# A two-part transformer kernel: expert weights in half-and-half slots with 512-column matmuls, gate slot first in the dense stages, and zero matmuls between stages

## The chip, the cores and the metric

One core of a Trainium2 chip (trn2) runs the whole program in one launch. The metric is the device time of one execution in microseconds (us). TensorE is called PE here, its weight loads PEld; VectorE is DVE, ScalarE is ACT, GpSimd is POOL, and SyncE (SP) issues the loads.

## What is computed

The input is x, 256 tokens of 1024 features, batch 1. The first block has two layers. Each layer is a feed-forward network, a mixer and a second feed-forward network, all of them behind an RMS norm whose shift, scale and output gate come from `silu(c) @ w_ada + b_ada` (nine vectors of 1024 per layer). The mixer of layer 0 is a differential attention of 4 heads beside a multiscale pooling; that of layer 1 is a short gated convolution. A feed-forward network is

```
x = x + 0.5 * g * ((silu(h @ wg) * (h @ wu)) @ wd)      # h = norm(x), wg, wu 1024 x 2816, wd 2816 x 1024
```

The second block has one layer: latent attention and block attention, two gates and an output projection, and then a mixture of experts: a router picks one of four groups for each token and two of the eight experts in it.

```
y[token] += weight * ((silu(h @ w_g[e]) * (h @ w_u[e])) @ w_d[e])   # w_g, w_u 1024 x 256, w_d 256 x 1024, 32 experts
```

A last norm gives the output. All data is float32.

## The kernel before

**Split precision.** Every product of a weight and an activation is three PE matmuls with float32r operands: high times high, high times low, low times high. ACT makes the high part of a weight tile (L1300, L1310, a copy to float32r), DVE the low part (L1678, L2213, raw minus high). PE needs both.

**Slots.** Weights go through three slots, s = 0, 1, 2, each with a raw tile, a high tile and a low tile of 128 x 2048 (1 MB). In a feed-forward network slot 0 holds a chunk of 256 columns of the gate weight, slot 1 the same of the up weight and slot 2 256 rows of the down weight; 11 chunks make a network. In the other dense stages unit u uses slot u mod 3. SP issues the load of a slot (`load`, L393 to L399) after it has waited until the previous content is split; semaphores `landed`, `high`, `split` and `used` count loads, high parts, low parts and matmuls done per slot. SP works through its loads in one written order, so that a load that waits holds those behind it. ACT and DVE also have written orders.

**Stages.** ffn0, mix0, ffn1, ffn2, mix1, ffn3, blk2, moe. ffn0 to ffn2 also load the 4 MB of w_ada for each vector in quarters (`ada_load`) and DVE reduces them (L1730). Ahead of each stage stands a norm: ACT squares x in four pairs of feature blocks as they become final (L1323), PE sums the squares over partitions with a matrix of ones (`norm_sums`, L683, matmuls at L690), ACT takes the root (L1329), DVE the reciprocal (L1744), and then for each of the eight feature blocks k of h: DVE scales (L1688), ACT makes hhi (L1337), DVE makes hlo (L1688 with hlo as output; L1772 where there is no shift) and counts `h_ready`.

**The start of a stage.** `first_two` (L603) does the first two units, or the first gate and up chunk. It waits for both slots before its first matmul. For each k, as h_ready comes, it does output half m=0 of slot 0 and of slot 1 (six matmuls of 256 columns); then half m=1 of slot 0 for all k (24 matmuls, then `used[0]`), and half m=1 of slot 1 (24 matmuls, then `used[1]`). In a feed-forward network 16 zero matmuls of 128 columns (L792) go ahead of it, which open the PSUM banks of the down product. After it the next gate chunk follows (L579 to L581 via `gate`), for which slot 0 must be refilled: ACT copies after `used[0]`, DVE subtracts, and only then does ACT apply silu to the first gate chunk.

**Loads ahead of ffn3.** The last four units of mix1 are in slots 0, 1, 2, 0. `chunk_loads` (L405) then loads the first gate chunk into slot 0 and after it the first up chunk into slot 1. ACT's `norm` (L1314 and on) makes high parts between the squares (`refill`, L1302): the last mix1 unit of slot 0, the first up chunk, the first down chunk; DVE makes the low parts between the output additions of mix1 (`add_units`, L1876 and on).

**The expert stage.** An expert's gate is in slot 0, its up in slot 1, its down in slot 2; the raw tiles exist twice (even and odd experts). `expert` (L490) issues three loads of 1 MB for each expert, in order gate, up, down, each with 8 KB contiguous per partition, after the split of the same slot two experts earlier. On PE an expert's tokens (128) are the stationary operand and the weights move. Per step (L1226 and on):

```
into_hidden(0, e + 1)    # gate: 8 row blocks x 3 matmuls of 256 columns, L1183 to L1185
hidden_turn(e)           # two transposes of silu * up, L1194
into_hidden(1, e + 1)    # up: 24 matmuls of 256 columns
out_of_hidden(e)         # down: 12 matmuls of 512 columns, L1208 to L1210
```

In three of eight steps of groups 1 to 3, `scatter` (L1223, L1224) adds 4 or 8 matmuls. ACT applies silu after `used[1]`, DVE multiplies by up and the slot weight.

## Time and profile before

| | us |
|---|---|
| median of 3 runs | 1722.42 (1721.34 to 1727.29) |
| the profiled execution, its own time | 1724.32 |
| its span | 1722.5 |
| PE busy in the span | 1609.0 |
| DVE busy | 1130.3 |
| ACT busy | 780.7 |
| moved by DMA | 379.90 MB |

The span is the time from the first to the last instruction of the profiled execution, and that execution's own time is 1.8 us more. A row of the timeline gives when an instruction starts and how long it lasts; matmuls overlap their successors, so what a matmul costs in a dense run is the distance from one start to the next and not its duration. In the windows view PEclk is the share of full speed that PE's clock was granted. Lines "L579" and so on are lines of the kernel above.

### The profile page before, as it was taken

Reading aid. Unit: us, or ns where it says so; the run is one execution under the profiler, and the core shown is the slowest. Engines: PE = TensorE matmul, PEld = TensorE weight load, DVE = VectorE, ACT = ScalarE, POOL = GpSimd, SP = SyncE. Lnnn points to the kernel's source line nnn. Section 1 sums busy time; section 2 is a strip of 40 time slices with the busy share of each in tenths; the row PEclk is TensorE's granted clock in tenths of the full one; section 3 lists DMA queues with packets and bytes.
Section 4 is the critical chain, followed back from the end, with each engine's and each line's share of the span. In section 5 each row is a group of like instructions: output and inputs, shape, how many; then the busy total and the mean of one; then the engine's idle time right before and its main releaser. Section 6 shows DMA issues by size and latency. Waiting matters only on the chain.

```text
span 1722.5 us, 29138 instructions
## 1 busy us (share of the span) xinstructions
PE 1609.0 (93%) x12267; PEld 1522.4 (88%) x12267; DVE 1130.3 (66%) x1156; ACT 780.7 (45%) x808; POOL 17.2 (1%) x24
## 2 busy tenths in 40 slices
PE   5999989789999999998988999899899889999995
PEld 3999988579999999998988999898788689999994
DVE  2777777567777677756645454664664568888983
ACT  2433344434333443334434333444454447777772
POOL 0000000300000000000000000000000000000000
PEclk8999999889999999999998999999999889999997
DMA  9897766336878587863625555354332518898980
GB/s 323 273 329 278 271 242 242 125 123 248 289 270 313 173 292 270 313 196 126 196 98 171 177 188 177 126 171 117 110 123 98 218 54 347 342 357 346 357 327 26
DMA packets 202482, 379.90 MB, mean 221 GB/s; under 512 B 12185, under 2 KB 157470, under 8 KB 190110
## 3 DMA queue, kind: packets, MB, share of 16 engines
q1 hardware_dynamic: 202398, 378.70, 62.4%
q8 instruction: 62, 1.02, 0.2%
q14 instruction: 22, 0.18, 0.0%
HBM read 377.63 MB, written 1.05 MB: 220 GB/s over the span
## 4 chain that ended last, share of the span: by engine, by line
PE 84%; DVE 7%; ACT 4%; DMA 3%; issue 1%; SPq 0%; ACTq 0%; DVEq 0%
PE ps L579 20%; PE ps L580 19%; PE ps L581 19%; PE ps L1183 3%; PE ps L1185 3%; PE ps L1184 3%; DVE wlo L1678 3%; ACT whi L1300 2%; PE ps L1208 2%; PE ps L1209 2%; PE ps L1210 2%; DMA ada_raw<-in_w_ada_dram 2%; PE ps L690 2%; DVE rstd L1744 1%; PE ps L705 1%
## 5 line engine op out<-in xcount | busy, mean ns | idle before, releaser
L1678 DVE TENSOR_TENSOR wlo<-raw,whi 128x2048 fp32r<-128x2048 f32 (+1 forms) x191 | 432.9, 2267 | 346.5 <-ACT whi L1300 346.4
L579 PE MATMUL ps<-hhi,whi 128*128 128x256 f32 (+1 forms) x2024 | 587.7, 290 | 27.8 <-DVE hlo L1688 16.7
L580 PE MATMUL ps<-hlo,whi 128*128 128x256 f32 (+1 forms) x2024 | 579.1, 286 | 0.0
L581 PE MATMUL ps<-hhi,wlo 128*128 128x256 f32 (+1 forms) x2024 | 578.7, 286 | 0.0
L1300 ACT ACTIVATE whi<-raw 128x2048 fp32r<-128x2048 f32 (+1 forms) x191 | 360.1, 1886 | 209.9 <-PE ps L581 164.2
L579 PEld LDWEIGHTS ps<-hhi,whi 128*128 128x128 f32 (+1 forms) x2024 | 395.1, 195 | 35.8 <-issue 26.5
L580 PEld LDWEIGHTS ps<-hlo,whi 128*128 128x128 f32 (+1 forms) x2024 | 395.1, 195 | 1.8 <-issue 1.4
L581 PEld LDWEIGHTS ps<-hhi,wlo 128*128 128x128 f32 (+1 forms) x2024 | 394.8, 195 | 0.0
L579 PE MATMUL ps<-hidhi,whi 128*128 128x256 f32 x704 | 201.0, 286 | 2.8 <-DVE wlo L1805 2.8
L581 PE MATMUL ps<-hidhi,wlo 128*128 128x256 f32 x704 | 199.2, 283 | 0.0
L580 PE MATMUL ps<-hidlo,whi 128*128 128x256 f32 x704 | 199.2, 283 | 0.0
L579 PEld LDWEIGHTS ps<-hidhi,whi 128*128 128x128 f32 x704 | 134.9, 192 | 9.4 <-issue 5.8
L580 PEld LDWEIGHTS ps<-hidlo,whi 128*128 128x128 f32 x704 | 135.0, 192 | 0.0
L581 PEld LDWEIGHTS ps<-hidhi,wlo 128*128 128x128 f32 x704 | 135.0, 192 | 0.0
L1730 DVE SCALAR_TENSOR_TENSOR arena<-ada_raw,cact,arena 128x1024 f32<-128x1024 f32 x98 | 125.8, 1284 | 3.4
L2213 DVE TENSOR_TENSOR wlo<-raw,whi 128x2048 fp32r<-128x2048 f32 x45 | 103.0, 2289 | 11.9 <-ACT whi L1310 11.0
L1365 ACT ACTIVATE hidhi<-act_tile 128x512 fp32r<-128x512 f32 x44 | 27.8, 632 | 169.8 <-DVE act_tile L1796 169.8
L1359 ACT ACTIVATE act_tile<-ps 128x512 f32<-128x512 f32 x44 | 26.3, 598 | 147.9 <-PE ps L581 147.8
L2213 DVE TENSOR_TENSOR wlo<-ada_raw,whi 128x2048 fp32r<-128x2048 f32 x32 | 73.3, 2291 | 24.1 <-ACT whi L1310 24.1
L579 PE MATMUL ps<-mhi,whi 128*128 128x256 f32 (+1 forms) x256 | 76.9, 300 | 12.4 <-DVE mlo L1899 8.8
L1310 ACT ACTIVATE whi<-raw 128x2048 fp32r<-128x2048 f32 x45 | 86.0, 1912 | 5.0 <-PE ps L1210 4.3
L580 PE MATMUL ps<-mlo,whi 128*128 128x256 f32 (+1 forms) x256 | 76.1, 297 | 0.0
(276 smaller groups left out, 2449.7 us busy)
## 6 DMA issues: line engine op xcount, KB each, us to landing
ada_raw<-in_w_ada_dram SPq DMA_DIRECT2D x72, 1024.0 KB, 5.3
raw<-in_ffn_wg_dram SPq DMA_DIRECT2D x44, 1024.0 KB, 5.6
raw<-in_ffn_wu_dram SPq DMA_DIRECT2D x44, 1024.0 KB, 5.4
raw<-in_ffn_wd_dram SPq DMA_DIRECT2D x44, 1024.0 KB, 6.8
raw<-in_w_in_dram SPq DMA_DIRECT2D x18, 1024.0 KB, 5.4
raw<-in_w_exp_gate_dram SPq DMA_DIRECT2D x16, 1024.0 KB, 6.6
raw<-in_w_exp_up_dram SPq DMA_DIRECT2D x16, 1024.0 KB, 8.6
raw<-in_w_exp_down_dram SPq DMA_DIRECT2D x16, 1024.0 KB, 4.8
```

The lines of the kernel that those rows point to most:

```text
L579: pe.matmul(o, wh, xh, start=start, stop=False, skip_group_check=shared)
L580: pe.matmul(o, wh, xl, start=False, stop=False, skip_group_check=shared)
L581: return pe.matmul(o, wl, xh, start=False, stop=stop, skip_group_check=shared)
L690: mm = pe.matmul(ps[:, 7, 0:T], ones, hf[:, k, :], start=(k == 0), stop=(k == KT - 1))
L1183: pe.matmul(o, hi[:, k, :], whi[s][:, c], start=(k == 0), stop=False)
L1184: pe.matmul(o, hi[:, k, :], wlo[s][:, c], start=False, stop=False)
L1185: mm = pe.matmul(o, lo[:, k, :], whi[s][:, c], start=False, stop=(k == KT - 1))
L1300: act.activation(whi[s][:, 0:width], raw[s][:, 0:width], ACT.Copy).then_inc(high[s], 1)
L1310: return act.activation(o, i, ACT.Copy, scale=scale)
L1678: dve.tensor_tensor(wlo[s][:, 0:width], raw[s][:, 0:width], whi[s][:, 0:width].bitcast(F32), ALU.subtract).then_inc(split[s], 1)
L1730: ins = dve.scalar_tensor_tensor(out=adasum, in0=w, scalar=weight, in1=adasum, op0=ALU.mult, op1=ALU.add)
L2213: dve.tensor_tensor(wlo[s][:, :], weights_of(s, p), whi[s][:, :].bitcast(F32), ALU.subtract).then_inc(split[s], 1)
```

## The change

It has five parts.

1. **Expert slots.** Slot 0 holds row blocks 0 to 3 of gate and of up, slot 1 row blocks 4 to 7 of both. Each of the two slots is loaded by two DMAs of 512 KB (4 KB contiguous per partition). A matmul of `into_hidden` now moves 512 columns: 256 of gate and 256 of up for one row block, into one PSUM bank. Slot 0 begins the sums and slot 1 ends them. The waits on `landed` and `landed_odd` count both DMAs.
2. **`first_two` by slots.** For each k both output halves of slot 0; `used[0]` after that loop. Then the wait for slot 1, and all 48 matmuls of slot 1.
3. **Zero matmuls.** `keep_clock(n, vectors)` behind `norm_sums` issues n matmuls of 256 columns with zero operands into a spare half bank: 30 ahead of mix0, mix1 and blk2, 18 ahead of ffn1, ffn2 and ffn3, none ahead of ffn0 and in the last norm.
4. **Load order of ffn3's first chunk.** Up (slot 1) is issued ahead of gate (slot 0).
5. For the first expert all the row blocks of both slots wait for their part of the gathered tokens (before, those of slot 0 alone).

```
--- before.py
+++ after.py
@@ -407,8 +407,8 @@
                 b = first[stage]
 
                 def pair(c):
-                    load(0, c + b[0], wg(c))
-                    load(1, c + b[1], wu(c))
+                    for s in ((1, 0) if stage == "ffn3" and isinstance(c, int) and c == 0 else (0, 1)):
+                        load(s, c + b[s], (wg, wu)[s](c))
 
                 def down(c):
                     load(2, c + b[2], wd(c))
@@ -489,16 +489,24 @@
 
             def expert(e, parity, src_e=None):
                 src_e = e if src_e is None else src_e
-                for s, w in enumerate((a["w_exp_gate_2"], a["w_exp_up_2"], a["w_exp_down_2"])):
+
+                def rows_of(w):
                     w = w[0, src_e] if isinstance(src_e, int) else w[0, bass.ds(src_e, 1)].rearrange("e k n -> (e k) n")
-                    w = w.rearrange("(p k) n -> p k n", p=P)
+                    return w.rearrange("(p k) n -> p k n", p=P)
+
+                for s in range(3):
+                    arrived = (landed_odd if parity else landed)[s]
                     if isinstance(e, int) and e == 0:
-                        load(s, b_moe[s], w)
+                        sp.wait_ge(split[s], b_moe[s])
+                    elif not isinstance(e, int) or e > 1:
+                        sp.wait_ge(split[s], e + (b_moe[s] - 1))
+                    if s == 2:
+                        w = rows_of(a["w_exp_down_2"])
+                        sp.dma_start(weights_of(s, parity).rearrange("p (k n) -> p k n", k=2), w).then_inc(arrived, 16)
                         continue
-                    if not isinstance(e, int) or e > 1:
-                        sp.wait_ge(split[s], e + (b_moe[s] - 1))
-                    sp.dma_start(weights_of(s, parity).rearrange("p (k n) -> p k n", k=w.shape[1]),
-                                 w).then_inc((landed_odd if parity else landed)[s], 16)
+                    halves = weights_of(s, parity).rearrange("p (w k n) -> p w k n", w=2, k=KT // 2)
+                    for i, w in enumerate((a["w_exp_gate_2"], a["w_exp_up_2"])):
+                        sp.dma_start(halves[:, i], rows_of(w)[:, 4 * s:4 * s + 4, :]).then_inc(arrived, 16)
 
             expert(0, 0)
             sp.wait_ge(sem("mixed"), 2)
@@ -600,27 +608,28 @@
                         mm = three(o, wh[:, k, c], wl[:, k, c], xh[:, k0_ + k, :], xl[:, k0_ + k, :], j == 0, j == nk - 1)
                 mm.then_inc(used[s], 1)
 
-            def first_two():
-
-                def product(s, k, m):
+            def first_two(second):
+
+                def product(s, k, m, start):
                     c = slice(k * 2 * P + m * P, k * 2 * P + (m + 1) * P)
                     return three(ps[:, s, m * T:(m + 1) * T], whi[s][:, c], wlo[s][:, c], hhi[:, k, :], hlo[:, k, :],
-                                 k == 0, k == KT - 1)
+                                 start, k == KT - 1, shared=True)
 
                 for k in range(KT):
                     wait("h_ready")
-                    for s in range(2):
-                        product(s, k, 0)
-                for s in range(2):
+                    for m in range(2):
+                        mm = product(0, k, m, k == 0 and m == 0)
+                mm.then_inc(used[0], 1)
+                second()
+                for m in range(2):
                     for k in range(KT):
-                        mm = product(s, k, 1)
-                    mm.then_inc(used[s], 1)
+                        mm = product(1, k, m, k == 0)
+                mm.then_inc(used[1], 1)
 
             def first_units(freed_by):
-                for s in range(2):
-                    slot_ready(s)
-                    own(s)
-                first_two()
+                slot_ready(0)
+                own(0)
+                first_two(second=lambda: (slot_ready(1), own(1)))
                 for s in range(2):
                     frees(s, freed_by[s])
 
@@ -680,7 +689,16 @@
 
             norms = [0]
 
-            def norm_sums():
+            def keep_clock(n, vectors):
+
+                if n:
+                    own(6)
+                    pe.wait_ge(sem("mod_ready"), vectors)
+                for _ in range(n):
+                    pe.matmul(ps[:, 6, T:2 * T], zeros[:, :], zeros[:, :].rearrange("p (o n) -> p o n", o=1).to_broadcast([P, 2, P]),
+                              start=True, stop=True)
+
+            def norm_sums(fill=0, vectors=0):
                 norms[0] += 1
                 counts["x_ready"] = 4 * norms[0]
                 own(7)
@@ -690,6 +708,7 @@
                     mm = pe.matmul(ps[:, 7, 0:T], ones, hf[:, k, :], start=(k == 0), stop=(k == KT - 1))
                 mm.then_inc(sem("stat_ready"), 1)
                 frees(7, "stat_read")
+                keep_clock(fill, vectors)
 
 
             def ada_quarter(r, n, v_before=None):
@@ -793,10 +812,13 @@
                 pe.wait_ge(split[0], b0[0] + 1)
                 if ch:
                     pe.wait_ge(sem("silu_done"), ch)
-                pe.wait_ge(split[1], b0[1] + 1)
-                if ch:
-                    pe.wait_ge(sem("hid_done"), ch)
-                first_two()
+
+                def second():
+                    pe.wait_ge(split[1], b0[1] + 1)
+                    if ch:
+                        pe.wait_ge(sem("hid_done"), ch)
+
+                first_two(second)
 
                 def pair(i, v=None):
 
@@ -866,7 +888,7 @@
                     rows = slice(64 * half, 64 * half + 64)
                     scores(2 * h + half, q0[rows, h, :], k0[rows, h, :])
 
-            norm_sums()
+            norm_sums(30, 7)
             first_units(("sq_done", "sq_done"))
             for u in range(8):
                 if 1 < u < 6:
@@ -961,22 +983,22 @@
                 for j in range(4):
                     linear(stage, u0 + j, "x_ready", mhi, mlo, ready if j == 0 else None)
 
-            norm_sums()
+            norm_sums(18, 9)
             chunked("ffn1", 9)
-            norm_sums()
+            norm_sums(18, 14)
             chunked("ffn2", 14, 4)
 
 
-            norm_sums()
+            norm_sums(30, 18)
             first_units(("evacuated", "v_done"))
             for u in range(2, 12):
                 linear("mix1", u, ("evacuated", "v_done", "y_done")[u % 3])
             outputs("mix1", 12, lambda k: wait("mix_split") if k % 2 == 0 else None)
-            norm_sums()
+            norm_sums(18, 18)
             chunked("ffn3")
 
 
-            norm_sums()
+            norm_sums(30, 18)
 
             def rope(r):
 
@@ -1175,14 +1197,15 @@
                 if s == 0 and (not isinstance(e, int) or e >= 2):
                     pe.wait_ge(sem("moe_hidden"), e - 1)
                 hi, lo = block_h(g)
-                o = ps[:, p, s * CH:(s + 1) * CH]
-                for k in range(KT):
-                    if isinstance(e, int) and e == 0 and s == 0:
+                o = ps[:, p, :]
+                wh, wl = (w[s][:, :].rearrange("p (w k n) -> p k w n", w=2, k=KT // 2) for w in (whi, wlo))
+                for j in range(KT // 2):
+                    k = KT // 2 * s + j
+                    if isinstance(e, int) and e == 0:
                         wait("gathered_split")
-                    c = slice(k * CH, (k + 1) * CH)
-                    pe.matmul(o, hi[:, k, :], whi[s][:, c], start=(k == 0), stop=False)
-                    pe.matmul(o, hi[:, k, :], wlo[s][:, c], start=False, stop=False)
-                    mm = pe.matmul(o, lo[:, k, :], whi[s][:, c], start=False, stop=(k == KT - 1))
+                    pe.matmul(o, hi[:, k, :], wh[:, j], start=(k == 0), stop=False, skip_group_check=True)
+                    pe.matmul(o, hi[:, k, :], wl[:, j], start=False, stop=False, skip_group_check=True)
+                    mm = pe.matmul(o, lo[:, k, :], wh[:, j], start=False, stop=(k == KT - 1), skip_group_check=True)
                 mm.then_inc(used[s], 1)
 
             def hidden_turn(e, p):
@@ -1303,6 +1326,8 @@
 
                 n = turn[s]
                 if n < len(widths[s]):
+                    if s < 2 and n == b_moe[s]:
+                        act.wait_ge(landed[s], (n + 2) * 16)
                     split_high(s, n, widths[s][n])
                     turn[s] += 1
 
@@ -1587,10 +1612,11 @@
             act.activation(rt[:, 64:72], rt[:, 56:64], ACT.Exp).then_inc(sem("router_exp"), 1)
             def expert_high(s, e, p):
 
+                each = 8 if s == 2 else 16
                 if p:
-                    act.wait_ge(landed_odd[s], e * 8 + 8)
+                    act.wait_ge(landed_odd[s], e * each + each)
                 else:
-                    act.wait_ge(landed[s], e * 8 + (b_moe[s] + 1) * 16)
+                    act.wait_ge(landed[s], e * each + (b_moe[s] * 16 + 2 * each))
                 act.wait_ge(used[s], e + b_moe[s])
                 copy(whi[s][:, :], weights_of(s, p)).then_inc(high[s], 1)
```

## Rows read from the trace of the kernel before

**Rows 1.** The page, busy time by engine, and the shares of the chain that ended last
```profile
PE 1609.0 (93%) x12267; PEld 1522.4 (88%) x12267; DVE 1130.3 (66%) x1156; ACT 780.7 (45%) x808; POOL 17.2 (1%) x24
...
PE 84%; DVE 7%; ACT 4%; DMA 3%; issue 1%; SPq 0%; ACTq 0%; DVEq 0%
```

**Rows 2.** Waits of PE over the span (who for whom: us in total, times, longest us)
```profile
PE ps L579 <- DVE hlo L1688: 16.7, 5, 4.1
...
PE ps L579 <- DVE wlo L1678: 7.3, 5, 1.6
...
PE ps L579 <- DVE hlo L1772: 3.9, 1, 3.9
```

**Rows 3.** Timeline, start of ffn2 (start us, us, engine, line, operation, tiles, count [idle before])
```profile
586.52 2.09 PE L792 MATMUL ps<-zeros 128*128 128x128 f32 x16
...
590.97 0.55 PE L579 MATMUL ps<-hhi,whi 128*128 128x256 f32 x1 [2.36 <-DVE hlo L1688]
...
595.76 0.48 DVE L1688 SCALAR_TENSOR_TENSOR hlo<-hf,modv,hhi 128x256 fp32r<-128x256 f32 x1 [0.18 <-ACT hhi L1337]
...
602.59 1.92 ACT L1300 ACTIVATE whi<-raw 128x2048 fp32r<-128x2048 f32 x1 [5.07 <-PE ps L581]
...
604.49 0.28 PE L579 MATMUL ps<-hhi,whi 128*128 128x256 f32 x1
...
604.54 2.29 DVE L1678 TENSOR_TENSOR wlo<-raw,whi 128x2048 fp32r<-128x2048 f32 x1 [4.69 <-ACT whi L1300]
...
604.85 0.28 PE L579 MATMUL ps<-hhi,whi 128*128 128x256 f32 x1
...
606.96 0.38 PE L579 MATMUL ps<-hhi,whi 128*128 128x256 f32 x1 [1.59 <-DVE wlo L1678]
```

**Rows 4.** Windows: us, busy (x) of PE PEld DVE ACT POOL, PEclk, DMA, GB/s
```profile
254.20:259.40 5.20, 5.20 (x25) 5.20 (x26) 5.02 (x13) 3.52 (x7) 0.00 (x0) 0.53 0.76 303
384.00:389.20 5.20, 5.20 (x31) 5.18 (x32) 5.02 (x13) 3.55 (x7) 0.00 (x0) 0.67 0.14 54
591.00:596.20 5.20, 5.20 (x24) 5.20 (x25) 5.02 (x13) 3.52 (x7) 0.00 (x0) 0.50 0.71 284
798.70:803.90 5.20, 5.20 (x32) 5.20 (x33) 5.02 (x13) 3.54 (x7) 0.00 (x0) 0.70 0.00 0
909.80:915.10 5.30, 5.28 (x27) 5.30 (x28) 5.11 (x13) 3.05 (x6) 0.00 (x0) 0.56 1.04 344
1112.60:1117.40 4.80, 4.79 (x28) 4.80 (x29) 4.65 (x13) 2.94 (x7) 0.00 (x0) 0.66 0.00 0
```

**Rows 5.** The same view, while ffn1's sixteen zero matmuls run
```profile
379.60:381.60 2.00, 1.99 (x18) 1.82 (x16) 1.13 (x1) 0.47 (x1) 0.00 (x0) 1.00 1.05 409
```

**Rows 6.** Timeline, the norm ahead of ffn3
```profile
893.66 1.91 ACT L1300 ACTIVATE whi<-raw 128x2048 fp32r<-128x2048 f32 x1 [10.28 <-DMA raw<-in_ffn_wu_dram]
...
896.18 1.91 ACT L1300 ACTIVATE whi<-raw 128x2048 fp32r<-128x2048 f32 x1
...
900.81 0.86 DVE L1688 SCALAR_TENSOR_TENSOR xT<-ps,modv,xT 128x256 f32<-128x256 f32 x2
```

**Rows 7.** Timeline of PE, one expert's period in the expert stage
```profile
1420.41 0.41 PE L1194 MATMUL ps<-cst,act_tile 128*128 128x128 f32 x2
...
1423.54 0.40 PE L1208 MATMUL ps<-whi,hidhi 128*128 128x512 f32 x1
...
1424.23 0.40 PE L1208 MATMUL ps<-whi,hidhi 128*128 128x512 f32 x1
...
1429.15 0.41 PE L1194 MATMUL ps<-cst,act_tile 128*128 128x128 f32 x2
```

**Rows 8.** Windows: two stretches with loads of expert weights, columns as in rows 4
```profile
1355.00:1360.00 5.00, 3.88 (x23) 3.26 (x23) 4.34 (x3) 3.58 (x4) 0.00 (x0) 1.00 1.01 423
1450.00:1680.00 230.00, 230.00 (x1634) 216.50 (x1632) 203.58 (x144) 165.66 (x131) 0.00 (x0) 1.00 0.89 347
```

**Rows 9.** Waits of ACT over the span
```profile
ACT whi L1310 <- DMA ada_raw<-in_w_exp_gate_dram: 4.8, 6, 1.3
```

## Prediction

> **What bounds the kernel now.** The page's busy times come first: PE is busy in 93% of the span, and the chain that ended last is 84% PE [rows 1]. Time can be won in three ways: PE's rare waits, stretches in which its clock is down, and cheaper instructions. The waits of PE come second [rows 2]. Five times, 16.7 us in all and 4.1 at most, PE waits for the first block of h behind a norm (blk2 has a sixth of 3.9), and five times, 7.3 us in all, for a low weight part; four of these are 1.6 us each, one behind `first_two` in each feed-forward network. Third is the timeline of ffn2's start [rows 3]: what lies before PE's first real matmul and what before the first one of the next chunk. Fourth are the windows in which h arrives [rows 4], where PEclk stands at 0.50 to 0.70. Last, one expert period [rows 7] beside DMA in that stage [rows 8]: there PE has no gap in 230 us, clock 1.00, DVE is busy 203.6 and DMA 0.89.
>
> **Unit prices.** At full speed three 256-column matmuls take 604.85 - 604.49 = 0.36 us, 0.12 each [rows 3]. At half clock the 24 matmuls of ffn2's 5.2 us cost 0.217 each [rows 4]. Three 512-column matmuls take 1424.23 - 1423.54 = 0.69, 0.23 each [rows 7]. As a check, an expert has 48 x 0.12 + 12 x 0.23 + 2 x 0.12 = 8.76, and the period is 1429.15 - 1420.41 = 8.74.
>
> **Part 1, expert slots.** 48 matmuls of 256 columns become 24 of 512: 5.76 - 24 x 0.23 = 0.24 saved; with 0.229 (0.69 over 3 is rounded) 0.26. It repeats for experts 1 to 31: 8.1 us. Expert 0 gains nothing: PE then waits for the router's chain on ACT and DVE. The Trainium skill, page "TensorE: Matmul & The Clock Gate", section "Back-to-back issue gap", gives a fixed 2.5 ns beside the columns at full clock; by it this part would bring 24 x 31 x 2.5 ns = 1.9 us (its figures worked out), and the rows, with 0.12 and 0.23, speak against that.
> Is PE still the bound? DVE has 203.6 of 230 [rows 8], 7.95 in a mean period of 8.98 (8.74, and 16 scatter matmuls of 0.12 in eight experts), and the new mean is 8.72. It fits, but ACT's and DVE's chains leave under a microsecond in the steps with scatters. DMA must carry 3.15 MB per period, 361 GB/s where it was 347 on average; 420 has been seen with the same loads [rows 8]. Runs of 4 KB: w_ada has such runs, and its stretch shows 409 GB/s at a share of 1.05 [rows 5], against 423 at 1.01 [rows 8], so 7% more engine time per byte for two thirds of the bytes: 0.89 x 1.047 x 8.98/8.72 = 0.96. That still fits, barely, and ACT already waited six times up to 1.3 us for a gate load [rows 9]. SP issues five DMAs per expert for three, on a queue with nothing else to do. I take 0.5 us off for new waits: **7.6**. The bounds are 8.1 and 0.
> The down load of expert 0 now stands behind four issues instead of two, and blk2's last norm waits for it. Two more issues hide behind the megabytes ahead of it in DMA; I take nothing, at most 0.5.
>
> **Part 2, gate slot first.** The matmuls are the same 96. But `used[0]` comes after the loop over k, with 48 matmuls (5.76 us) still to do, instead of 24 (2.88). What follows it is ACT 1.92 and DVE 2.29 [rows 3], 4.2 in all, which 2.88 did not cover and 5.76 does, even behind the down slot's high part, which ACT makes first. The last group of three of `first_two` starts at 604.85, so the next chunk could start at 605.21, and it starts at 606.96: 1.75 us, in ffn0 to ffn3: **7.0**. The next thing due is the up slot's refill after `used[1]`; it needs about the 5.76 us of the next gate chunk, so it is late by 0.1 at most. Bounds: 5.5 to 7.0.
>
> **Part 3, zero matmuls.** In ffn2 PE idles 2.36 us ahead of the first block [rows 3], in the mixers 4.1, in blk2 3.9 [rows 2]. With zeros of 0.12 each, 18 are 2.16 and 30 are 3.6: both end ahead of the first block, so they delay nothing by themselves. What they may give: at full clock PE does six matmuls (0.72) per block and keeps up with blocks that come every 0.75 (596.24 - 590.97 over seven) [rows 3], so 42 are done when the eighth arrives. In the windows it did 25, 31, 24, 32, 27 and 28 [rows 4]. The shortfall times 0.12 is 2.0, 1.3, 2.2, 1.2, 1.8 and 1.7. For ffn2 I can count exactly, the eighth block starts at 595.76, and 0.48 + 54 x 0.12 = 6.96 later is 602.72, against 605.21: 2.5. Sum 10.5. Do zero operands hold the clock? No row shows it alone. The nearest: during sixteen zero matmuls ahead of ffn1 the clock stayed 1.00 [rows 5], and it fell only after the gap. I take yes for five stages. In ffn3 DVE makes the gate slot's low part ahead of the blocks (2.3 us more), so 18 zeros leave a gap like ffn2's, which cost the clock: minus 1.5. **9.0**; bounds 0 and 10.5.
> The same page's section on the clock gate says that PE idle time brings the half clock and activity the full one; by that rule the gain comes as worked out, but it does not say whether zeros count.
>
> **Part 4, ffn3's first loads.** ACT waits 10.28 us for the up load, until 893.66, and then copies the down slot at 896.18 [rows 6]. The low part of that copy (2.29 [rows 3]) lies on DVE directly ahead of the last output addition at 900.81, on which the norm depends. With up issued first, its copy is over long before; down lands where up did, and its copy starts at 893.7. All behind it moves by 896.18 - 893.66 = **2.5**, until PE's own end of mix1 binds. The gate load, now second, is needed only behind the norm. Bounds 1.5 to 3.
>
> **Sum.** 7.6 + 7.0 + 9.0 + 2.5 = 26.1. The profiled execution took 1724.3 (span 1722.5), so 1698.2. The median is 1.9 lower: **1696**.
>
> **Rivals.**
> A. Zero operands do not hold the clock. For: a zero tile may not count as work, and only 2 us of it were seen. Against: the clock in [rows 5]. Without part 3 the time is 1696 + 9 = 1705.
> B. In the expert stage DMA binds. For: 0.96 worked out, and the six waits [rows 9]. Against: 423 GB/s [rows 8]. Part 1 brings nothing: 1704. The skill's page "DMA: Bandwidth & Descriptors", section "Specifications", gives a limit of about 358 GB/s per core; with it a period can't go below 8.79 and part 1 brings 0.19 x 31 = 6, so 1698. The 423 here speaks against the limit.
> C. DMA moves half slots at the pace of a stretch with short runs, such as mix0's start, 303 GB/s at 0.76, or 344 at 1.04 ahead of ffn3 [rows 4]. At 325 GB/s an expert takes 9.68 and the stage grows by 31 x 0.7 = 22, more than the 18.5 of the dense parts: 1726, slower. It decides from 3.15 MB in 9.58 us, 328 GB/s; at 303 it would be 1747. Against it: 409 with 4 KB runs [rows 5].
> D. Gate first does not cover the refill, since silu's table load and the down slot's copy stand in ACT's queue ahead; parts 2 and 3 then give half of theirs: 1704.
>
> **How the numbers follow.** The forecast gets 0.66, A 0.12, B 0.12, C 0.03, D 0.07. From the forecast's own range (1691 with every bound good, 1700 with waits in several places) to A, B and D, the range is 1690 to 1706; beyond lie A with B (1713), C, and half of B's and A's spread. A measurement here tells 0.5%, 8.6 us, from no change, so faster means under 1713.8: the forecast, A, B and D, with a little taken off, 0.93; same 0.05; slower 0.02.
>
> **What the profile after would show.** Right: waits for the low part of about zero behind `first_two`, not 7.3; clock 1.00 in the windows of the first blocks of all but ffn0 and ffn3; the eighth block 6.96 us ahead of the next unit's first matmul; a period of 8.48 between the hidden turns; DMA share near 0.95; ACT's wait for up gone ahead of ffn3. Wrong: PE idle at 24 matmuls per expert with waits for DMA (B, C); clock 0.5 to 0.7 right behind zeros (A); a wait for gate's low part of over 0.3 (D).

## The result, and the profile after

| | before | after |
|---|---|---|
| median, us (runs) | 1721.34 (7) | 1711.9 (7, 1705.38 to 1721.58) |
| the profiled execution, its own time | 1724.32 | 1708.61 |
| its span | 1722.5 | 1706.8 |

The change makes the kernel faster, by less than forecast: the ratio to the kernel before is 0.9939, with a 95% interval of 0.9912 to 0.9967. That is about 10 us (0.61% of 1721), where the forecast had 26; 1711.9 lies outside the range of 1690 to 1706. Line numbers moved: L579 to L581 are now L587 to L589, L1678 is L1704, L1688 is L1714, L1300 is L1323, L1183 to L1185 are L1206 to L1208, L2213 is L2239, L1310 is L1335.

The page first, its busy times and its chain, against [rows 1]:

```profile
PE 1605.9 (94%) x11643; PEld 1482.9 (87%) x11643; DVE 1129.0 (66%) x1156; ACT 780.4 (46%) x808; POOL 17.2 (1%) x24
...
PE 73%; DVE 10%; DMA 8%; ACT 4%; issue 3%; SPq 1%; ACTq 0%; DVEq 0%
```

PE's share of the span hardly moved, but its share of the chain fell from 84% to 73%, and DMA's rose from 3% to 8%. Something that used to run beside PE is now on the path. The waits say where. Of PE:

```profile
PE ps L1206 <- DVE wlo L2239: 10.0, 13, 2.0
...
PE ps L587 <- DVE hlo L1714: 3.9, 5, 2.4
...
PE ps L587 <- DVE wlo L1704: 0.9, 1, 0.9
...
PE ps L587 <- DVE hlo L1798: 0.3, 1, 0.3
```

Of ACT:

```profile
ACT whi L1335 <- DMA ada_raw<-in_w_exp_up_dram: 18.4, 23, 2.3
ACT whi L1335 <- DMA raw<-in_w_exp_up_dram: 16.9, 24, 2.1
...
ACT whi L1323 <- DMA raw<-in_w_exp_down_dram: 10.3, 1, 10.3
```

The last three rows of the first fence answer to [rows 2], and all three shrank: 16.7 us became 3.9, 7.3 became 0.9, 3.9 became 0.3. The first row is new. PE waits in the expert stage, where it had no gap, for a low part, which waits for ACT, which waited 47 times, 35.3 us in all, for an up load. In [rows 9] it was 4.8 us in six waits, for gate loads (and 1.9 us in six more for up loads). The 0.9 left of the 7.3 is the fifth wait, which was 0.9 before too; the four behind `first_two` are gone.

The windows in which h arrives, columns as in [rows 4], which they answer in the same order (the last reaches from the first blocks of blk2 to the eighth):

```profile
251.25:256.45 5.20, 5.20 (x40) 5.09 (x41) 5.02 (x13) 3.54 (x7) 0.00 (x0) 1.00 0.76 302
378.72:383.92 5.20, 5.20 (x40) 5.10 (x41) 5.02 (x13) 3.53 (x7) 0.00 (x0) 1.00 0.16 64
582.86:588.06 5.20, 5.20 (x40) 5.11 (x41) 5.02 (x13) 3.53 (x7) 0.00 (x0) 1.00 0.70 280
787.23:792.43 5.20, 5.20 (x40) 5.11 (x41) 5.02 (x13) 3.53 (x7) 0.00 (x0) 1.00 0.00 0
894.16:899.36 5.20, 5.20 (x30) 5.18 (x31) 5.02 (x13) 3.06 (x6) 0.00 (x0) 0.67 1.04 340
1094.70:1099.50 4.80, 4.73 (x39) 4.76 (x40) 4.65 (x13) 2.88 (x7) 0.00 (x0) 1.00 0.00 0
```

Five of six stand at a granted clock of 1.00 with 39 or 40 matmuls in place of 24 to 32. The fifth, ffn3, stands at 0.67 with 30 (27 before). Both are what was forecast; the exception in ffn3 proves to be chance below (part 3). 1.00 is the full level, 2.4 GHz, and 0.50 the half, 1.2 GHz; a value between them is the mean of a window that holds both. The start of ffn2, against [rows 3]:

```profile
578.39 2.50 PE L698 MATMUL ps<-zeros 128*128 128x256 f32 x18
...
582.84 0.36 PE L587 MATMUL ps<-hhi,whi 128*128 128x256 f32 x1 [0.21 <-DVE hlo L1714]
...
587.62 0.48 DVE L1714 SCALAR_TENSOR_TENSOR hlo<-hf,modv,hhi 128x256 fp32r<-128x256 f32 x1 [0.18 <-ACT hhi L1362]
```

PE's idle time ahead of the first block is 0.21 us, where it was 2.36. From the eighth block on, every third matmul starts 0.36 us after the last, without a gap, past 594.6, where the next chunk begins by count (587.62 + 0.48 + 54 x 0.12). That is 7.0 us behind the eighth block, and it was 11.2. The norm ahead of ffn3, against [rows 6]:

```profile
880.61 1.92 ACT L1323 ACTIVATE whi<-raw 128x2048 fp32r<-128x2048 f32 x1 [5.23 <-DMA raw<-in_ffn_wd_dram]
...
884.77 0.87 DVE L1714 SCALAR_TENSOR_TENSOR xT<-ps,modv,xT 128x256 f32<-128x256 f32 x2
```

ACT now waits 5.2 us for the down load and no longer 10.3 for the up load ahead of it, and the last output addition follows the down copy directly.

**By stages.** From the reciprocal of one norm to that of the next, before and after, us:

| stretch | before | after | difference | forecast |
|---|---|---|---|---|
| ffn0 | 227.4 | 225.6 | -1.8 | -1.75 |
| mix0 | 129.8 | 127.5 | -2.3 | -2.0 |
| ffn1 | 207.0 | 204.1 | -2.9 | -3.1 |
| ffn2 | 207.7 | 204.4 | -3.3 | -4.2 |
| mix1, norm ahead of ffn3 | 109.0 | 104.7 | -4.2 | -3.7 |
| ffn3 | 205.2 | 203.0 | -2.2 | -2.0 |
| blk2 | 255.4 | 253.2 | -2.2 | -1.7 |
| expert stage to the last norm | 346.8 | 350.8 | **+4.1** | **-7.6** |

The dense stretches together gave 18.9 us, and 18.5 were forecast. The spans of the two profiled executions are 15.7 us apart, 10.4 less than forecast, and the last row alone is 11.7 off: the whole miss between them lies there. The medians are only 9.4 apart, because the changed kernel's executions scatter by 16 us, with the clock: 1705.38 was reached at a mean granted clock of 0.973, 1721.58 at 0.960. For the same reason two rows say less than they seem to. The kernels below that share ffn0's code take 225.4 to 228.5 us there, and e1 and e7, whose code for blk2 is the same, take 249.6 and 255.1, so that the close agreement in these two rows is partly luck.

### The profile page after: what moved, and what is told of

The parts are those of the page before. It is cut to its first block, busy times and chain, and to the rows that moved or that the text cites. A ratio compares the mean times of both kernels' runs of the same rounds, so it can differ in the third digit from the quotient of the medians.

```text
span 1706.8 us, 28052 instructions
## 1 busy us (share of the span) xinstructions
PE 1605.9 (94%) x11643; PEld 1482.9 (87%) x11643; DVE 1129.0 (66%) x1156; ACT 780.4 (46%) x808; POOL 17.2 (1%) x24
## 4 chain that ended last, share of the span: by engine, by line
PE 73%; DVE 10%; DMA 8%; ACT 4%; issue 3%; SPq 1%; ACTq 0%; DVEq 0%
PE ps L587 21%; PE ps L589 20%; PE ps L588 20%; DVE wlo L2239 4%; DMA ada_raw<-in_w_exp_up_dram 3%; DMA raw<-in_w_exp_up_dram 3%; DVE wlo L1704 2%; PE ps L708 2%; ACT whi L1335 2%; DMA ada_raw<-in_w_ada_dram 2%; ACT whi L1323 1%; DVE rstd L1770 1%; PE ps L724 1%; PE ps L1183 1%; PE ps L1206 1%
## 5 line engine op out<-in xcount | busy, mean ns | idle before, releaser
L1704 DVE TENSOR_TENSOR wlo<-raw,whi 128x2048 fp32r<-128x2048 f32 (+1 forms) x191 | 432.8, 2267 | 319.5 <-ACT whi L1323 319.3
L587 PE MATMUL ps<-hhi,whi 128*128 128x256 f32 (+1 forms) x2024 | 584.5, 289 | 5.1 <-DVE hlo L1714 3.9
L589 PE MATMUL ps<-hhi,wlo 128*128 128x256 f32 (+1 forms) x2024 | 574.4, 284 | 0.0
L1323 ACT ACTIVATE whi<-raw 128x2048 fp32r<-128x2048 f32 (+1 forms) x191 | 360.0, 1886 | 195.2 <-PE ps L589 154.5
L587 PEld LDWEIGHTS ps<-hhi,whi 128*128 128x128 f32 (+1 forms) x2024 | 389.9, 193 | 13.1 <-issue 10.3
L588 PEld LDWEIGHTS ps<-hlo,whi 128*128 128x128 f32 (+1 forms) x2024 | 390.1, 193 | 1.8 <-issue 1.4
L589 PEld LDWEIGHTS ps<-hhi,wlo 128*128 128x128 f32 (+1 forms) x2024 | 389.9, 193 | 0.0
L587 PE MATMUL ps<-hidhi,whi 128*128 128x256 f32 x704 | 201.0, 286 | 2.8 <-DVE wlo L1831 2.8
L589 PE MATMUL ps<-hidhi,wlo 128*128 128x256 f32 x704 | 199.2, 283 | 0.0
L587 PEld LDWEIGHTS ps<-hidhi,whi 128*128 128x128 f32 x704 | 135.0, 192 | 9.4 <-issue 5.8
L589 PEld LDWEIGHTS ps<-hidhi,wlo 128*128 128x128 f32 x704 | 135.0, 192 | 0.0
L2239 DVE TENSOR_TENSOR wlo<-raw,whi 128x2048 fp32r<-128x2048 f32 x45 | 103.0, 2288 | 18.6 <-ACT whi L1335 18.5
L1335 ACT ACTIVATE whi<-raw 128x2048 fp32r<-128x2048 f32 x45 | 86.2, 1915 | 20.3 <-DMA raw<-in_w_exp_up_dram 16.9
L2239 DVE TENSOR_TENSOR wlo<-ada_raw,whi 128x2048 fp32r<-128x2048 f32 x32 | 73.3, 2290 | 25.9 <-ACT whi L1335 25.8
L587 PE MATMUL ps<-mhi,whi 128*128 128x256 f32 (+1 forms) x256 | 75.4, 295 | 12.9 <-DVE mlo L1925 8.8
L589 PE MATMUL ps<-mhi,wlo 128*128 128x256 f32 (+1 forms) x256 | 74.5, 291 | 0.0
```

What stands on the lines that cost most here:

```text
L587: pe.matmul(o, wh, xh, start=start, stop=False, skip_group_check=shared)
L588: pe.matmul(o, wh, xl, start=False, stop=False, skip_group_check=shared)
L589: return pe.matmul(o, wl, xh, start=False, stop=stop, skip_group_check=shared)
L1323: act.activation(whi[s][:, 0:width], raw[s][:, 0:width], ACT.Copy).then_inc(high[s], 1)
L1335: return act.activation(o, i, ACT.Copy, scale=scale)
L1704: dve.tensor_tensor(wlo[s][:, 0:width], raw[s][:, 0:width], whi[s][:, 0:width].bitcast(F32), ALU.subtract).then_inc(split[s], 1)
```

## The experiments

The times in this section are medians of 5 to 12 runs. The ratios are to runs of the kernel before on the same chip (medians 1721.6, 1724.8 and 1722.6 in the three groups of runs), with their 95% intervals. An interval is 3 to 5 us to either side, so the difference of two ratios is uncertain by some 6 us, and smaller effects are read from stretches of the profiled executions. "Hidden turns" is the time from the first to the last transposition of an expert's hidden block, 31 periods; before it is 275.6 us and after 281.9. The five traces with the old expert stage in the old order (before, e1, e5, e6, e7) have 275.6 to 278.3, so a difference under 3 us says nothing. Rows of a run carry the line numbers of its own kernel.

The theory behind the first group: in the expert stage the weights arrive too late, either because of the order in which SP issues them (T1a) or because of the pace of the 4 KB runs (T1b).

**e1_old_experts: part 1 undone, parts 2 to 4 kept.**

```diff
-                    halves = weights_of(s, parity).rearrange("p (w k n) -> p w k n", w=2, k=KT // 2)
-                    for i, w in enumerate((a["w_exp_gate_2"], a["w_exp_up_2"])):
-                        sp.dma_start(halves[:, i], rows_of(w)[:, 4 * s:4 * s + 4, :]).then_inc(arrived, 16)
+                    sp.dma_start(weights_of(s, parity).rearrange("p (k n) -> p k n", k=w.shape[1]),
+                                 w).then_inc((landed_odd if parity else landed)[s], 16)
```

> The changed kernel with the expert stage as it was before: one 1 MB load per slot, 48 matmuls of 256 columns and 12 of 512 per expert; parts 2, 3 and 4 of the change stay. Theory T1 (the delivery of the expert weights became the bound, and part 1 costs time): the stretch from the last norm to the end goes back from 350.8 to about 346.7 us, the period between the hidden turns to 8.74, and the time falls to about 1703 (the dense parts alone gave 18.9 of stage time, 1721.3 - 18.9 = 1702.4), 5 to 9 us under the changed kernel. Rival (the expert stage is longer because the dense stages end earlier, with part 1 itself neutral): no change against the changed kernel, about 1710.

Measured: 1703.7, ratio 0.9899 (0.9875 to 0.9922), hidden turns 276.2, PE busy 229.6 of 230 us. Part 1 costs the changed kernel 0.0040 x 1722 = 6.9 us by the ratios, 8.2 by the medians, 5.7 in the hidden turns. By the ratios alone that is barely clear of the uncertainty of 6 us; with e2 the rival (part 1 neutral) falls.

**e2_experts_alone: the kernel before with part 1 alone.**

> The kernel before with part 1 of the change alone (half row blocks in 4 KB runs, matmuls of 512 columns). T1: the expert stage is 4 to 8 us longer than before, the time is 1725 to 1729, ACT waits for up loads as in the changed kernel (some 2 us, about 40 times), DMA share above 0.9. Rival (part 1 gains as predicted when it is alone, and only collides with the other parts): 1714.

Measured: 1728.5, ratio 1.0036 (1.0017 to 1.0055), hidden turns 286.0. Part 1 alone is slower, by 6.2 us (2.9 to 9.5), so it doesn't need the other parts to do harm.

**e3_early_loads: the changed kernel, with another order of issue on SP.**

```diff
-            expert(1, 1)
-            with sp.Fori(0, (NE - 2) // 2) as i:
+            expert(1, 1, slots=(0, 1))
+            def early(e, parity):
+                expert(e, parity, slots=(0, 1))
+                expert(e - 1, 1 - parity, slots=(2,))
+            early(2, 0)
+            early(3, 1)
+            with sp.Fori(0, (NE - 4) // 2) as i:
                 for half in range(2):
-                    expert(i * 2 + 2 + half, half)
+                    early(i * 2 + 4 + half, half)
+            expert(NE - 1, 1, slots=(2,))
```

> The changed kernel, but SP issues the two half slots of expert e ahead of the down load of expert e-1, so a freed gate or up buffer is asked for without standing behind a down load whose buffer comes free last. Same bytes, same runs. T1a (the order of issue and the landing time of 8 us bound two periods): the waits for up loads shrink, the period falls toward 8.5 to 8.6, the time to 1697 to 1704. T1b (the pace of the 4 KB runs itself binds, DMA engines near 1.0): it stays at 1707 to 1713 with DMA share 0.93 to 1.0 and the waits only move to the down loads.

Measured: **1691.7**, ratio 0.9845 (0.9818 to 0.9872), hidden turns 266.4. The same bytes, in the same runs, by the same number of DMAs, 20 us under the changed kernel by the medians, 16 by the ratios. Two turns of its timeline, a window in the middle of the stage, and under it the same view of the changed kernel:

```profile
1501.17 0.39 PE L1224 MATMUL ps<-cst,act_tile 128*128 128x128 f32 x2
...
1509.62 0.39 PE L1224 MATMUL ps<-cst,act_tile 128*128 128x128 f32 x2
```

```profile
1400.00:1630.00 230.00, 230.00 (x1057) 191.33 (x1056) 211.38 (x148) 169.87 (x137) 0.00 (x0) 1.00 0.98 365
```

```profile
1420.00:1650.00 230.00, 222.24 (x1001) 179.79 (x1000) 196.95 (x140) 161.44 (x129) 0.00 (x0) 1.00 0.93 341
```

The period is 8.45 us, PE has no gap, and the waits of ACT list no load of an expert after the first. DMA works at a share of 0.98 and 365 GB/s. The changed kernel's PE idles 7.8 of 230 us while its DMA stands at 0.93 and 341 GB/s, so DMA had capacity left there. T1b, pace alone, falls: the weights came late because they were asked for late.

**The mechanism, in three timelines.** In the kernel before (SPq rows are the issues of DMAs, whi rows copies of a slot on ACT, wlo rows low parts on DVE):

```profile
1502.91 2.29 DVE L2213 TENSOR_TENSOR wlo<-raw,whi 128x2048 fp32r<-128x2048 f32 x1
...
1509.29 2.29 DVE L2213 TENSOR_TENSOR wlo<-arena,whi 128x2048 fp32r<-128x2048 f32 x1
...
1511.61 0.33 SPq L500 DMA_DIRECT2D arena<-in_w_exp_down_dram  x1
...
1512.47 0.33 SPq L500 DMA_DIRECT2D raw<-in_w_exp_gate_dram  x1
...
1519.50 1.91 ACT L1310 ACTIVATE whi<-raw 128x2048 fp32r<-128x2048 f32 x1
```

The gate buffer is free at 1502.91 + 2.29 = 1505.20, but SP asks for the next gate load only at 1512.47, because the down load ahead of it in the queue waits for its own buffer until 1511.58. That leaves 1519.50 - 1512.47 = 7.0 us to land in; the median landing was 6.7 (below). It just fitted. In the changed kernel:

```profile
1511.37 0.33 SPq L509 DMA_DIRECT2D raw<-in_w_exp_gate_dram  x1
...
1511.79 0.38 SPq L509 DMA_DIRECT2D raw<-in_w_exp_up_dram  x1
...
1520.06 0.33 SPq L505 DMA_DIRECT2D raw<-in_w_exp_down_dram  x1
...
1520.64 0.33 SPq L509 DMA_DIRECT2D ada_raw<-in_w_exp_gate_dram  x1
...
1521.15 1.92 ACT L1335 ACTIVATE whi<-raw 128x2048 fp32r<-128x2048 f32 x1 [2.07 <-DMA raw<-in_w_exp_up_dram]
...
1525.45 0.50 PE L1206 MATMUL ps<-whi,mhi 128*128 128x512 f32 x1 [1.38 <-DVE wlo L2239]
```

ACT is ready for slot 0 at 1521.15 - 2.07 = 1519.08, 7.3 us behind the issue of its second half. The half lands 9.4 us behind its issue. ACT is 2.07 late, the down copy that stands behind on ACT is late with it, its low part frees the down buffer late, and the next burst of five issues starts late. As these rows read, the delay feeds the next one; it does not grow without end, for the plain periods lie between 8.45 and 10.3 us. In e3:

```profile
1489.51 0.33 SPq L509 DMA_DIRECT2D ada_raw<-in_w_exp_gate_dram  x1
...
1489.95 0.36 SPq L509 DMA_DIRECT2D ada_raw<-in_w_exp_up_dram  x1
...
1494.47 0.33 SPq L505 DMA_DIRECT2D raw<-in_w_exp_down_dram  x1
...
1501.96 1.91 ACT L1342 ACTIVATE whi<-ada_raw 128x2048 fp32r<-128x2048 f32 x1
```

The halves are issued 4.5 us ahead of the down load, and have 1501.96 - 1489.95 = 12.0 us to land in. The medians of issue to landing, of three kernels in turn, the changed one, e3 and e1 (the last number of each row of the page's list of DMA issues):

```profile
raw<-in_w_exp_gate_dram SPq DMA_DIRECT2D x32, 512.0 KB, 6.5
raw<-in_w_exp_up_dram SPq DMA_DIRECT2D x32, 512.0 KB, 7.7
...
ada_raw<-in_w_exp_up_dram SPq DMA_DIRECT2D x32, 512.0 KB, 8.4
```

```profile
raw<-in_w_exp_gate_dram SPq DMA_DIRECT2D x32, 512.0 KB, 4.8
raw<-in_w_exp_up_dram SPq DMA_DIRECT2D x32, 512.0 KB, 6.5
```

```profile
raw<-in_w_exp_gate_dram SPq DMA_DIRECT2D x16, 1024.0 KB, 6.5
raw<-in_w_exp_up_dram SPq DMA_DIRECT2D x16, 1024.0 KB, 8.7
```

These rows mix the halves of both slots. For slot 0 alone, the medians over experts 1 to 31 are, for this and for the runs below:

| kernel | issue of slot 0's last load to ACT being ready for it, us | its landing, us | waits of ACT for it |
|---|---|---|---|
| before | 7.1 | 6.7 | 6 |
| e1 | 7.2 | 6.7 | 6 |
| changed | 6.8 | 7.5 | 24 |
| e4 | 6.7 | 7.5 | 19 |
| e11 | 7.2 | 7.6 | 13 |
| e3 | 12.5 | 6.4 | 0 |
| e12 | 13.0 | 6.5 | 0 |
| e9 | 13.6 | 5.1 | 0 |

Slot 0 needed one gate load before, and that landed just in time. It now needs a second load too, which is issued 0.4 us behind the first and lands in 7.5 us, where 6.8 are left.

**e4_old_4k: e1 with each gate and up load as two DMAs in 4 KB runs.**

```diff
-                    sp.dma_start(t, w).then_inc(arrived, 16)
+                    for i in range(2):
+                        sp.dma_start(t[:, 4 * i:4 * i + 4, :], w[:, 4 * i:4 * i + 4, :]).then_inc(arrived, 16)
```

> As e1_old_experts (matmuls of 256 columns, gate in slot 0 and up in slot 1), but each gate and up load is issued as two DMAs of 512 KB in 4 KB runs in place of one of 1 MB in 8 KB runs. T1b (the runs or the number of loads slow the delivery): longer than e1_old_experts by 4 to 10 us, ACT waiting for loads, DMA share above 0.93. T1c (what costs is that the first slot needs a half of gate and a half of up at once, or the strided matmuls, not the runs): within 1.5 us of e1_old_experts.

Measured: 1714.3, ratio 0.9957 (0.9938 to 0.9975), 10.6 us over e1 by the medians; hidden turns 286.0, PE busy 224.0 of 230. So even with the old matmuls and a slot 0 that holds gate alone, issuing the same bytes in five smaller DMAs costs as much as part 1 was to bring, and slot 0's last load is late 19 times. The strided 512-column matmuls (T1c) are not the cause.

**e12_4k_early: e4 with e3's order of issue.**

> As e4_old_4k (two DMAs of 512 KB in 4 KB runs per gate and up slot, matmuls of 256 columns), with the order of issue of e3_early_loads. T1 (slower delivery costs time only through loads that stand behind a down load in the queue): as e1_old_experts again, 1703 to 1706, period 8.74, no wait of ACT for an expert load. Rival (the order helps only the half slots, by what each slot needs): 1709 or more.

Measured: 1704.0, ratio 0.9893 (0.9869 to 0.9918), hidden turns 275.9, every plain period 8.74. The order cures e4 completely, down to e1's time.

**e9_old_early: e1 with e3's order of issue.**

> As e1_old_experts (one load of 1 MB in 8 KB runs per slot, matmuls of 256 columns), with the order of issue of e3_early_loads: the gate and up loads of expert e ahead of the down load of expert e-1. It completes the square of slot form and order. T1 (order matters only where the delivery is late; PE had no gap in e1_old_experts): within 2 us of e1_old_experts, about 1703, period 8.74. Rival (the order of issue is a gain by itself, and what e3_early_loads showed is not part 1): 5 us or more under e1_old_experts.

Measured: 1705.7, ratio 0.9891 (0.9861 to 0.9921), hidden turns 275.1. The order alone brings nothing where nothing was late. With it, e9 against e3 is part 1 alone with the delivery out of the way: 275.1 to 266.4, **8.7 us** gained, against the 8.1 of the prediction's upper bound; 0.3 of it lies in the first period, which waits for the router's chain.

**e11_one_4k: e1 with 4 KB runs, but one DMA per slot.** The rows of gate and up are taken in another order than those of h, so these products are over other pairs of rows.

```diff
+                        w = rows.rearrange("(h p k) n -> p h (k n)", h=2, p=P)
+                        t = t.rearrange("p (h x) -> p h x", h=2)
                     sp.dma_start(t, w).then_inc((landed_odd if parity else landed)[s], 16)
```

> As e1_old_experts (three DMAs of 1 MB per expert, matmuls of 256 columns, order of issue as before), but from expert 1 on each gate and up load takes its rows as two runs of 4 KB per partition from two halves of the matrix, in one DMA. The rows then stand in another order than those of h, so these products are over other pairs of rows; work and bytes are the same. If the 4 KB runs alone slow the delivery: as e4_old_4k, about 1714, with ACT waiting for gate loads and PE under 226 of 230 us. If the number of DMAs does it: as e1_old_experts, 1703.

Measured: 1705.3, ratio 0.9902 (0.9876 to 0.9928), hidden turns 278.4. The shorter runs do lengthen the landing, from 6.7 to 7.6 us, and ACT waits 13 times in place of 6, but 278.4 against e1's 276.2 is within the scatter of that stage (e5, with 8 KB runs, has 278.3). The split in two DMAs costs 7.6 us (286.0 against 278.4), clear of it: the landing is as long, and the second load is issued later, so that 6.7 us are left in place of 7.2. The old order has no slack for either. e1 and e11 also differ in which rows of DRAM a run covers; that was not separated.

**e8_old_2x8k: e1 with two DMAs per slot, each for 64 of the 128 partitions.**

```diff
+                        sp.dma_start(t[64 * i:64 * i + 64], w[64 * i:64 * i + 64]).then_inc(arrived, 16)
```

> As e4_old_4k (two DMAs of 512 KB per gate and up slot, matmuls of 256 columns, order of issue as before), but each DMA takes 64 of the 128 partitions, so that its runs stay 8 KB long. If the length of the runs is what slows the delivery: as e1_old_experts, about 1703. If the number of DMAs is (five issues per expert in place of three): as e4_old_4k, about 1714.

Measured: 1839.0, ratio 1.0653 (1.0621 to 1.0685). Neither expectation held, and the run can't tell runs from number, because it changed a third thing. A window of it:

```profile
1420.00:1650.00 230.00, 173.52 (x1068) 157.22 (x1067) 131.81 (x93) 108.09 (x87) 0.00 (x0) 0.90 0.95 233
```

DMA is as busy as ever (0.95) and moves 233 GB/s in place of e1's 351. Per byte the engines are busy 1.6 times as long (0.95 / 233 against 0.90 / 351), though a third of the bytes, the down loads, still goes into all 128 partitions at a time. PE idles a quarter of the time.

**e10_down0_first: e3, and the down load of expert 0 issued first.**

```diff
-            expert(0, 0)
+            expert(0, 0, slots=(2, 0, 1))
```

> As e3_early_loads, and SP issues the down load of expert 0 ahead of its gate and up halves, right when its buffer comes free (some 14 us earlier). In e3_early_loads ACT waits 9.9 us for that load, and the output additions of the last dense stage and the last norm stand behind it. If that wait holds the last norm up: the wait is gone, the reciprocal of the last norm comes 4 to 5 us earlier, the time is 1687. Rival (PE's own products bound the end of that stage, and ACT's wait was slack): as e3_early_loads, 1692.

Measured: **1688.4**, ratio 0.9791 (0.9765 to 0.9816), the fastest of all. In e3 the down load is issued at 1325.96, though its buffer was long free, and ACT waits for it:

```profile
1333.16 1.92 ACT L1330 ACTIVATE whi<-raw 128x2048 fp32r<-128x2048 f32 x1 [9.89 <-DMA raw<-in_w_exp_down_dram]
...
1343.20 1.75 DVE L1777 RECIPROCAL rstd<-root 128x256 f32<-128x256 f32 x1 [2.39 <-ACT root L1361]
```

and in e10:

```profile
1310.38 0.34 SPq L505 DMA_DIRECT2D raw<-in_w_exp_down_dram  x1
...
1337.94 1.75 DVE L1775 RECIPROCAL rstd<-root 128x256 f32<-128x256 f32 x1 [3.27 <-ACT root L1359]
```

The wait is gone, and the last norm comes 5.3 us earlier. In the expert stage behind it 2.5 us are lost again (333.3 in e3, 335.8 here, to the next reciprocal). The medians differ by 3.3, the profiled spans by 2.9, and the ratios by 0.0054, 9 us, each with an interval of about 0.0026 either way, so its worth beside e3 is given as 3 to 9.

**e5_no_zeros: e1 without the zero matmuls of part 3.**

> As e1_old_experts without the zero matmuls of part 3 in all six places. By the prediction's step (zeros hold the clock, PE then keeps up with the blocks of h) it is 9.0 slower, 1712.7, with granted clocks of 0.5 to 0.7 in the stretches of the first blocks. Rival A (the zeros do nothing and gate first alone cured the waits for h): as e1_old_experts, 1703.7.

Measured: 1711.2, ratio 0.9916 (0.9889 to 0.9943). Its windows, the first four of those above:

```profile
252.51:257.71 5.20, 5.20 (x24) 5.20 (x25) 5.01 (x13) 3.53 (x7) 0.00 (x0) 0.50 0.76 304
383.03:388.23 5.20, 5.20 (x30) 5.18 (x31) 5.02 (x13) 3.53 (x7) 0.00 (x0) 0.67 0.17 64
588.37:593.57 5.20, 5.20 (x31) 5.20 (x32) 5.02 (x13) 3.53 (x7) 0.00 (x0) 0.67 0.73 286
793.21:798.41 5.20, 5.20 (x31) 5.20 (x32) 5.02 (x13) 3.53 (x7) 0.00 (x0) 0.67 0.00 0
```

Without the zeros the clock is at 0.50 to 0.67 again and 24 to 31 matmuls are done, where there were 40. Rival A falls as a mechanism. The size is less sharp: 7.6 us by the medians, 2.9 by the ratios, 7.7 in the stretches from mix0 to ffn3 of its profiled execution (2.8, 1.1, 0.5, 1.5 and 1.8), which was the slowest of its six. In blk2 it is 4.5 over e1, which says nothing, since e7, with the zeros, is 5.5 over e1 there.

**e6_both_slots: e1 with part 2 undone.**

> As e1_old_experts with part 2 undone: the first two slots of each network in turn over k, as before; the zero matmuls stay. By the prediction's step: four refills are late again by 1.75 us, so 7.0 slower than e1_old_experts, and four waits of PE for the low part behind those matmuls come back at about 1.6 us each. Rival (gate first and the zeros cover the same idle time, so that one without the other gives little): less than 3 us or more than 10 slower.

Measured: 1711.4, ratio 0.9933 (0.9910 to 0.9955): 7.7 us over e1 by the medians, 5.9 by the ratios, and 1.7 in each of ffn1 and ffn2, where 1.75 was forecast. The other stretches are disturbed by the clock: ffn3 is 2.7 longer, but e1 kept a clock of 1.00 in its window there and e6 did not (0.69), which is worth 1.2 of it (below, part 3); mix1 is 1.3 longer; and ffn0 is 1.6 shorter, where e6's first blocks ran at 1.00 and e1's at 0.65. The waits came back as they were:

```profile
PE ps L579 <- DVE wlo L1688: 7.3, 5, 1.6
```

**e7_gate_load_first: e1 with part 4 undone.**

> As e1_old_experts with part 4 undone: the first gate load of ffn3 is issued ahead of the up load, as before. By the prediction's step the reciprocal of the norm ahead of ffn3 comes 2.5 us later behind ACT's wait for the up load, and the time is 2.5 slower. Rival (the end of that mixer is bound by PE): no change.

Measured: 1709.7, ratio 0.9921 (0.9902 to 0.9941): 6.0 us over e1 by the medians, 3.8 by the ratios. The stretch that ends with the norm ahead of ffn3 is 107.8 against 104.8, so 3.0 of it lie where they were expected. The two profiled executions differ by more, 10.3 us of span, and 5.5 of that lie in blk2 (255.1 against 249.6), whose code is the same: the mean granted clock is 0.96 there, and 0.99 in e1. ACT's queue again holds the down copy behind the wait for the up load:

```profile
882.22 1.92 ACT L1314 ACTIVATE whi<-raw 128x2048 fp32r<-128x2048 f32 x1 [11.33 <-DMA raw<-in_ffn_wu_dram]
...
884.60 1.92 ACT L1314 ACTIVATE whi<-raw 128x2048 fp32r<-128x2048 f32 x1
```

## Why the prediction was wrong, and where it was right

**Part 1 is the step that failed.** The prediction had 7.6 us gained with bounds of 8.1 and 0; in the changed kernel it costs 6.9 by the ratios of e1, 6.2 alone (e2). The swing of about 14.5 us is the miss of 1711.9 against 1696 but for 1.4, less than the scatter of the executions.

- The price of the matmuls was right. Period 8.48 was forecast and 8.45 is seen in e3; e9 against e3 gives 8.7 us, where 8.1 was the upper bound. The formula of the Trainium skill ("TensorE: Matmul & The Clock Gate", "Back-to-back issue gap") by which a matmul taken alone has 2.5 ns beside its columns would give 1.9 us; the runs don't agree with it for these matmuls, which each come with a weight load of their own: 8.74 - 8.45 = 0.29 us over 24 fewer is 12 ns each.
- The capacity of DMA was judged about right. 0.96 was worked out for the engines' share, and e3 has 0.98. That the two figures meet is in part luck: e9, with 8 KB runs in the same order, already has 0.96, so that the share doesn't tell what the short runs cost. "That still fits, barely" is true of the throughput. The Trainium skill's figure of about 358 GB/s per core ("DMA: Bandwidth & Descriptors", "Specifications"), by which rival B's part was worked out, is exceeded in e3, with 365 over 230 us and PE never waiting.
- What was wrong is the half sentence "SP issues five DMAs per expert for three, on a queue with nothing else to do". A queue with nothing else to do still has an order. SP reached the loads of an expert only when the down load ahead of them had got its buffer, 7.3 us after the gate buffer came free. The time from issue to ACT being ready was 7.1, and the landing took 6.7. Neither was looked up, though both could be read in the trace of before. The change made them 6.8 and 7.5. The six waits of [rows 9] were the sign that this distance had no slack. They were entered as 0.5 us.
- So the lower bound of 0 was too kind. "Nothing below zero" holds for a gain that is merely hidden; here the change made each slot depend on two loads in place of one, and that alone brings the loss, whatever the halves hold (e4), so that a loss was open. Rival C had the sign, but priced it by the pace of short runs, which was not what happened.

**Rival B** (DMA binds in the expert stage, 1704) named the right stage, with the wrong mechanism and a bound at zero. **Rival C** is refuted as it was put: at 365 GB/s the half slots move faster than anything needed. **Rivals A and D** fall by e5 and by the wait of 0.9 us for the low part behind the first two units.

**Part 2** (7.0): shown by e6, 1.7 each in the two undisturbed stretches and 5.9 to 7.7 in all, and by the waits that went from 7.3 to 0.9 and back to 7.3.

**Part 3** (9.0): the mechanism is shown by the windows, 40 matmuls where 42 were forecast; in all eleven kernels with the zeros the clock is 1.00 in the five windows outside ffn3. The exception of ffn3 was luck. The gap behind the zeros there is 2.42 us in every one of the eleven, and the clock in the window is 0.67 to 0.69 in six of the traces (the changed kernel, e3, e4, e6, e9, e12) and 1.00 in five (e1, e7, e8, e10, e11). The row of e1:

```profile
895.28:900.48 5.20, 5.20 (x40) 5.10 (x41) 5.02 (x13) 3.06 (x6) 0.00 (x0) 1.00 1.05 344
```

What it is worth is the 1.2 us between the two lengths of ffn3, 203.0 and 201.8, where the prediction took off 1.5. The size of part 3 is open between 3 and 8; parts 2 to 4 together, e1 against before, gave 18.0 by the medians and 17.4 by the ratio, against 18.5.

**Part 4** (2.5): 3.0 in the stretch where it was expected. The larger difference of the medians, 6.0, is not part 4's as far as the traces show: the rest of it is of the size by which blk2 differs between executions, with its clock.

**The down load of expert 0** "behind four issues instead of two": taken as nothing, at most 0.5. Its wait rose from 9.2 to 10.3 us, and it is issued 0.88 us after the low part of slot 1 frees the load ahead of it, and 0.42 in e1. So the two more issues cost the 0.5 of the bound, but the load also lands in 7.6 us in place of 6.9, which was not in the estimate: 1.1 in all. What was passed over is that the wait itself, 9.2 us in the kernel before, was the same case as part 4: a load that stands behind others whose buffers come free later. Turning it round (e10) moved its norm by 5.3 us, and part 4 moved its own by 3.0.

## What to carry to other kernels

Where one queue issues loads for several buffers, read three times of each load in the trace, when its buffer came free, when it was issued and when its data were first wanted, before changing the size or the number of the loads. A share of DMA under 1 and a sufficient GB/s say nothing of a load that is asked for late: the distance from issue to use must exceed the landing time, and a change that makes one consumer wait for two loads takes its slack from there. Put in the queue first what comes free first; here that turned a loss of 7 us into a gain of 9.

## What the runs showed of the hardware that was not expected

- With the gate and up loads as DMAs into 64 of the 128 partitions, same bytes and same 8 KB runs, 233 GB/s were moved at a DMA share of 0.95, where DMAs into all 128 moved 351 at 0.90 (e8 and e1).
- A gate load of 1 MB landed in 6.7 us in 8 KB runs (e1) and 7.6 in 4 KB runs of other rows (e11); as two DMAs of 512 KB in 4 KB runs the second landed 7.5 us behind its own issue (e4). The 31 periods took 276.2, 278.4 and 286.0 us. With the loads issued early the difference between the forms is under 1 us (275.1 in e9, 275.9 in e12).
- Zero matmuls that end 0.2 to 0.5 us ahead of the first block of h keep the granted clock at 1.00 through the eight blocks, in all 55 windows of eleven kernels. After 3.0 to 4.6 us of idle time it was 0.50 to 0.70 in all twelve windows of the kernels without part 3 (before, e2, e5). After 2.4 us of idle time it went either way, with or without the zeros of part 3 ahead of it: 0.50 to 0.69 in eleven windows, 1.00 in six.
